# Transposing x tiles by DMA instead of on TensorE, and reordered loads, in a one-layer hybrid decoder on eight cores

## What is computed

```python
def rmsnorm(x, g):
    xf = x.astype(jnp.float32)
    y = xf * lax.rsqrt(jnp.mean(xf * xf, axis=-1, keepdims=True) + EPS)
    return (y * g.astype(jnp.float32)).astype(x.dtype)
...
    proj = jnp.einsum("btd,de->bte", xn, w_in)          # xn = rmsnorm(x, norm_attn_g), w_in 1024 x 3072
    q, k, v, gate_b, gate_c, h = jnp.split(proj, SPLITS, axis=-1)
    # three attention groups of four heads of 64: windows 128, 512, 2048 with dilations 1, 4, 16
    # group outputs weighted by their softmax denominators; beside them a gated convolution of width 3
    mixed = jnp.concatenate([attn, conv_out], axis=-1)  # [B,T,1024]
    return jnp.einsum("bte,ed->btd", mixed, w_out), new_kv, new_conv
...
        x = x + mix
        x = x + squared_relu_mlp(rmsnorm(x, norm_mlp_g[l]), w_up[l], w_down[l])   # d_ff = 4096
    y = rmsnorm(x, norm_final_g)
```

## Time and profile before

| | |
|---|---|
| median of 3 runs | 3103.34 us (3100.91 to 3105.41) |
| the profiled execution's own time | 3103.4 us |
| its span, slowest core (core 1) | 3102.0 us |
| spans of the 8 cores | 3090.5 to 3102.0 us |
| mean granted TensorE clock of the cores | 0.984 to 0.986 |
| PE busy | 2953.4 us (95%) |
| DVE busy | 1302.3 us (42%) |
| ACT busy | 1032.7 us (33%) |
| POOL busy | 198.5 us (6%) |

### The profile page before, as it was taken

One profiled execution on the slowest core, in us unless ns is written; L12 is line 12 of the kernel. 1 busy time (PEld: TensorE's weight loads), 2 busy tenths in 40 slices (PEclk: granted clock), 3 DMA queues, 4 the chain that ended last, 5 costly groups with the idle time before them and its releaser, 6 DMA issues.

```text
span 3102.0 us, 62901 instructions; the slowest of 8 cores (3090.5 to 3102.0 us)
## 1 busy us (share of the span) xinstructions
PE 2953.4 (95%) x21987; PEld 1875.4 (60%) x21987; DVE 1302.3 (42%) x2876; ACT 1032.7 (33%) x2336; POOL 198.5 (6%) x256
## 2 busy tenths in 40 slices
PE   4997899999996899999999999999999999999998
PEld 2564465564553466666666666666666666666665
DVE  5445537548443333433343333433343333333332
ACT  3244336346243322322232323222232323222232
POOL 2201201101000000000000000000000000000000
PEclk9998999999998899999999999999999999999999
DMA  7414535435135646575655655565556665544320
GB/s 166 76 47 103 126 70 145 109 78 147 32 132 173 182 104 141 138 144 125 138 129 142 144 127 134 136 144 127 136 132 145 137 131 129 136 125 97 112 68 25
DMA packets 347119, 374.71 MB, mean 121 GB/s; under 512 B 209248, under 2 KB 301440, under 8 KB 343424
## 3 DMA queue, kind: packets, MB, share of 16 engines
q1 hardware_dynamic: 268832, 216.20, 27.5%
q0 software_dynamic: 71312, 67.19, 14.1%
q10 hardware_dynamic: 6672, 87.31, 8.7%
HBM read 309.57 MB, written 176.39 MB: 157 GB/s over the span
## 4 chain that ended last, share of the span: by engine, by line
PE 87%; DVE 4%; DMA 3%; issue 3%; ACT 2%; POOL 1%; SPq 1%; another core or an unknown queue 0%; DVEq 0%; ACTq 0%; POOLq 0%
PE pp L717 29%; PE pp L728 29%; PE pp L570 13%; PE pp L678 7%; PE pp L537 4%; DMA attnT<-xn 1%; PE pp L540 1%; DMA w_in_sb<-w_in 1%; PE pp L586 1%; PE pp L515 1%; DVE Csb L970 1%; DVE xn L918 1%; DVE Csb L967 1%; PE pp L607 1%; PE pp L590 1%
## 5 line engine op out<-in xcount | busy, mean ns | idle before, releaser
L717 PE MATMUL pp<-xn1T,w_up_sb 128*128 128x256 bf16 (+1 forms) x8448 | 1067.2, 271 | 1.8 <-DVE osb L1010 1.0
L728 PE MATMUL pp<-w_down_sb,h1T 128*128 128x512 bf16 x4160 | 1052.8, 379 | 0.2 <-DVE h1T L1130 0.2
L717 PEld LDWEIGHTS pp<-xn1T,w_up_sb 128*128 128x128 bf16 x8448 | 811.8, 98 | 284.5 <-issue 11.1
L876 ACT ACTIVATE hr<-pp 128x256 bf16<-128x256 f32 (+1 forms) x1056 | 393.3, 381 | 1163.7 <-PE pp L717 1129.9
L1130 DVE TENSOR_TENSOR h1T<-hr 128x256 bf16<-128x256 bf16 (+1 forms) x1056 | 300.8, 290 | 943.7 <-ACT hr L876 882.0
L728 PEld LDWEIGHTS pp<-w_down_sb,h1T 128*128 128x128 bf16 x4160 | 403.8, 98 | 287.4 <-issue 0.3
L570 PE MATMUL pp<-xnT,w_in_sb 128*128 128x512 bf16 x2304 | 536.6, 382 | 22.5 <-DMA w_in_sb<-w_in 9.9
L570 PEld LDWEIGHTS pp<-xnT,w_in_sb 128*128 128x128 bf16 x2304 | 212.4, 98 | 267.1 <-issue 35.0
L678 PE MATMUL pp<-w_out_sb,attnT 128*128 128x512 bf16 x1040 | 249.1, 383 | 4.2 <-DMA attnT<-xn 4.2
L840 ACT ACTIVATE PT<-pp 128x1024 bf16<-128x1024 f32 x171 | 174.7, 1024 | 120.3 <-PE pp L590 118.3
L1003 DVE TENSOR_TENSOR PT<-PT,mask 128x1024 bf16<-128x1024 bf16 (+1 forms) x192 | 129.4, 674 | 187.4 <-ACT PT L840 172.0
(11 more groups left out here) (130 smaller groups left out, 1751.7 us busy)
## 6 DMA issues: line engine op xcount, KB each, us to landing
kvs<-ck ACTq DMA_DIRECT2D x128, 510.0 KB, 4.7
xt<-xp SPq DMA_DIRECT2D x64, 512.0 KB, 4.9
xtB<-xp SPq DMA_DIRECT2D x64, 512.0 KB, 4.8
yp<-xtB SPq DMA_DIRECT2D x64, 512.0 KB, 4.3
NZ<-osb SPq DMA_DIRECT2D x192, 130.0 KB, 2.0
NZt<-NZ SPq DMA_DIRECT2D x64, 390.0 KB, 6.1
kvs<-ck ACTq DMA_DIRECT2D x32, 504.0 KB, 4.3
sK<-ck POOLq DMA_DIRECT2D x52, 256.0 KB, 4.0
```

The lines of the kernel that those rows point to most:

```text
L717: ins = e.matmul(bank(v % 2)[:, 0:N], lhsT=w_up_sb[:, i // 8, kc, (i % 8) * 128:(i % 8 + 1) * 128], rhs=xn1T[T % 2][:, kc, 0:N], start=kc ...
L728: ins = e.matmul(psD[s][:, half * 512:(half + 1) * 512], lhsT=h1T[v % NH][:, s * 128:(s + 1) * 128], rhs=w_down_sb[:, i, half * 512:(half ...
L876: e.activation(out=hr[v % NHR][:, 0:N], in_=bank(v % 2)[:, 0:N], func=AF.Relu).then_inc(s_hr, 1)
```

## The change

1. x tiles from the 18th on (`k >= 17`, 48 of them) are no longer transposed on TensorE and copied by VectorE; SyncE issues a DMA transpose (`xt`) from `xn` straight into `xnT`, once the projections ahead of it in the list have ended. The reader functions `x_read` and `x_ready` wait for it, and VectorE waits for the transpose of tile k-2 before it writes `xn` again.
2. `norm_attn_g` is multiplied into the weights `w_in_sb` instead (`gw`, 8 multiplies of 128x768 for each of the four arrays, on VectorE). The first 17 tiles keep their TensorE transpose, with a plain copy behind it.
3. ScalarE squares into `junkA` instead of into `xn`; to make room, `osb` has four buffers instead of five.
4. x tiles from the 5th on are loaded only when the first `w_in` array has landed; the second array is loaded at tile 6 instead of at the start.
5. The 16 stores of `kvss` of a group become one.
6. `w_out` is loaded in group 1 of the last round; the first quarter of `w_up` later in group 2. GpSimd waits for the first two `cvT` loads before it issues the other three quarters and `w_down`.
7. For pairs 0 and 1, `attn_n` and `xn1` are transposed by TensorE (`bp`, `tp`) into PSUM bank 0 or 7; ScalarE copies the first into `attnT`, VectorE multiplies the second straight from PSUM.

```diff
 FIRST_B = [(-1, "LX", 0, 0), (-1, "LX", 0, 1), (-1, "LN", 0, 0), (0, "LN", 0, 1), (0, "LC", 0, 0), (0, "a", 0, 0),
-           (1, "b", 0, 0), (2, "LN", 1, 0), (3, "a", 0, 1), (4, "b", 0, 1), (5, "c", 0, 0, 0), (5, "LN", 1, 1),
-           (6, "c", 0, 0, 1), (8, "c", 0, 1, 0), (9, "n", 0, 0), (9, "t", 0, 0), (10, "c", 0, 1, 1), (12, "d", 0, 0),
-           (13, "n", 0, 1), (13, "t", 0, 1), (15, "d", 0, 1)]
+           (2, "bp", 0, 0), (2, "LN", 1, 0), (3, "a", 0, 1), (4, "c", 0, 0, 0), (5, "bp", 0, 1), (5, "LN", 1, 1),
+           (6, "c", 0, 0, 1), (8, "c", 0, 1, 0), (9, "n", 0, 0), (10, "c", 0, 1, 1), (11, "tp", 0, 0), (11, "d", 0, 0),
+           (13, "n", 0, 1), (14, "tp", 0, 1), (14, "d", 0, 1)]
...
     def xb(self, k):
+        if k < 17:
+            self.steps.append(("xb", dict(k=k, n=self.nring)))
...
+        else:
+            self.steps.append(("xt", dict(k=k, full=self.nproj)))
...
+            for w, first in ((1, 16), (2, 32), (3, 48)):
+                if first <= P.slot < first + 8:
+                    P.add("gw", w=w, kc=P.slot - first)
...
+            if st == 3 and g == 1:
+                P.first_wo = P.nproj
+                P.later(3, "wl", i=0)
             if st == 3 and g == 2:
                 P.first_w = P.nproj
-                P.later(3, "wl")
+                P.later(20, "wl", i=1)
...
-    NO = 5
+    NO = 4
...
+        def x_ready(W, n):
+            W.wait_ge(s_xnT, min(n, 17))
+            for i in range(max(17, n - 2), n):
+                x_read(W, i)
...
+                            if n == 4:
+                                W.wait_ge(s_gw[0], kc + 1)
...
             elif what == "skv":
-                W.wait_ge(s_stkvs, 16 * 16 * a["g"])
+                W.wait_ge(s_stkvs, 16 * a["g"])
...
                     if k >= 2:
-                        W.wait_ge(s_xT, k - 1)
-                    e.activation(out=xn[k % 2][:], in_=xt[k % 4][:], func=AF.Square,
+                        W.wait_ge(s_xn, k - 1)
+                    e.activation(out=junkA[:], in_=xt[k % 4][:], func=AF.Square,
...
-                    e.tensor_tensor(out=xnTs[:] if k == 16 else xnT[:, :, col0:col0 + 128],
-                                    in0=bank_bf(a["n"] % 2).rearrange("p (k t) -> p k t", k=8),
-                                    in1=g_attn_sb[:, :].unsqueeze(2).broadcast_to([128, 8, 128]),
-                                    op=ALU.mult).then_inc(s_xnT, 1)
+                    e.tensor_copy(out=xnTs[:] if k == 16 else xnT[:, :, col0:col0 + 128],
+                                  in_=bank_bf(a["n"] % 2).rearrange("p (k t) -> p k t", k=8)).then_inc(s_xnT, 1)
+                elif kind == "gw":
...
+                    e.tensor_scalar(out=w_in_sb[w][:, kc, :], in0=w_in_sb[w][:, kc, :], scalar1=g_attn_sb[:, kc:kc + 1],
+                                    scalar2=None, op0=ALU.mult).then_inc(s_gw[w], 1)
                 elif kind == "xn":
                     k = a["k"]
                     W.wait_ge(s_rstd, k + 1)
+                    if k >= 2:
+                        x_read(W, k - 2)
...
+            for i in range(2):
+                W.wait_ge(s_bcv[i], 16)
             for c in range(1, 4):
                 e.dma_start(out=w_up_sb[:, c, :, :], in_=w_up_v[:, :, c * 1024:(c + 1) * 1024]).then_inc(s_wu[c], 16)
...
                 if kind == "xl":
                     k = a["k"]
+                    W.wait_ge(s_ldw[0], 16)
                     W.wait_ge(s_xn, k - 3)
...
+                elif kind == "xt":
+                    k = a["k"]
+                    col0 = (XSEQ[k] % 16) * 128
+                    W.wait_ge(s_xn, k + 1)
+                    W.wait_ge(s_proj, a["full"])
+                    e.dma_start_transpose(out=xnT[:, :, col0:col0 + 128], in_=xn[k % 2][:]).then_inc(s_xTd[k % 2], 16)
...
                     W.wait_ge(s_free[a["eng"]], a["first"])
-                    for bb in range(NSB):
-                        e.dma_start(out=kvs[g][bb, WIN[g] - 8:WIN[g], :], in_=kvss[bb * 8:(bb + 1) * 8, :]).then_inc(s_stkvs, 16)
+                    e.dma_start(out=kvs[g][:, WIN[g] - 8:WIN[g], :], in_=kvss[:]).then_inc(s_stkvs, 16)
```

More of the change, by code:

```diff
@@ L187, in make_plan @@
             P.xb(k - 1)
+    for kc in range(8):
+        P.add("gw", w=0, kc=kc)
     xs_conv = spread(4, 16, 0, 14)
@@ L453, in build_nc @@
         s_ldx = [sem("ld_x%d" % i) for i in range(4)]
+        s_xTd = [sem("x_tr%d" % i) for i in range(2)]
+        s_gw = [sem("w_in_scaled%d" % i) for i in range(4)]
         s_norm, s_rstd, s_xn, s_xT, s_xnT = sem("norm_chain"), sem("rstd"), sem("xn"), sem("xT"), sem("xnT")
@@ L522, in tensor_a @@
                         W.wait_ge(s_free[eng], v)
[L523 removed]
+                    x_ready(W, a["xb"])
                     wi = w_in_sb[0] if what[-1] in "BCHu" else w_in_sb[1 + a["g"]]
[L525 to L528 removed]
+                    w = 0 if what[-1] in "BCHu" else 1 + a["g"]
+                    W.wait_ge(s_gw[w], 8 if n > 4 else 1)
                     if what in ("v", "kvt"):
@@ L637, in order_b @@
                             continue
+                        elif what in ("b", "t", "bp", "tp") and (T + dT < 2) != (what[-1] == "p"):
+                            continue
                         elif 0 <= T + dT < NT_B and (not i or i[0] < nsub(T + dT)) and (T + dT > 1 or what != "LN"):
@@ L649, in b_bank, with tr_bank @@
             return 1 if T == 0 else B_M
+        def tr_bank(T):
+            return bank_bf(7 if T else 0).rearrange("p (k t) -> p k t", k=8)
         def tr_done(W, sems, q):
-            W.wait_ge(sems[q % 2], 16 * (q // 2 + 1))
+            if q < 4:
+                W.wait_ge(s_aTe if sems is s_aT else s_xTp, q + 1)
+            else:
+                W.wait_ge(sems[q % 2], 16 * (q // 2 - 1))
         def done_x1(T):
@@ L661, in tensor_b @@
             for kind, T, i, *half in events:
-                if kind == "c":
+                if kind == "bp":
+                    q = nsubs_before(T) + i
+                    if T == 0:
+                        W.wait_ge(s_free["act"], P.nev["act"])
+                        W.wait_ge(s_free["dve"], P.nev["dve"])
+                    W.wait_ge(s_an, q + 1)
+                    if q:
+                        W.wait_ge(s_aTe, q)
+                    for kc in range(6):
+                        ins = e.transpose(out=tr_bank(T)[:, kc, :], in_=attn_n[:, kc * 128:(kc + 1) * 128], identity=ident[:])
+                    ins.then_inc(s_aTp, 1)
+                elif kind == "tp":
+                    q = nsubs_before(T) + i
+                    W.wait_ge(s_xn1, q + 1)
+                    W.wait_ge(s_aTe, 2 * T + 2)
+                    if q:
+                        W.wait_ge(s_xn1T, q)
+                    for kc in range(8):
+                        ins = e.transpose(out=tr_bank(T)[:, kc, :], in_=xn1[:, kc * 128:(kc + 1) * 128], identity=ident[:])
+                    ins.then_inc(s_xTp, 1)
+                elif kind == "c":
                     q = nsubs_before(T) + i
@@ L865, in scalar_b @@
                 n = NORM.get((kind, T, i))
-                if kind == "c" and half[0] == 1:
+                if kind == "bp":
+                    q = nsubs_before(T) + i
+                    W.wait_ge(s_aTp, q + 1)
+                    if q >= 2:
+                        W.wait_ge(s_m, 2 * (q - 1))
+                    e.activation(out=attnT[q % 2][:, 0:6, :], in_=tr_bank(T)[:, 0:6, :], func=AF.Copy).then_inc(s_aTe, 1)
+                elif kind == "c" and half[0] == 1:
                     q = nsubs_before(T) + i
@@ L1120, in vector_b @@
                     W.wait_ge(s_ldgm, 16)
-                    e.tensor_tensor(out=xr, in0=xr,
+                    e.tensor_tensor(out=xr, in0=tr_bank(T) if q < 4 else xr,
                                     in1=g_mlp_sb[:, :].unsqueeze(2).broadcast_to([128, 8, 128]), op=ALU.mult
@@ L1216, in pool @@
             for kind, a in STEPS:
-                if kind == "xc" and a["k"] in (13, 16):
-                    load_w_in(1 if a["k"] == 13 else 2)
+                if kind == "xc" and a["k"] in (6, 13, 16):
+                    load_w_in((6, 13, 16).index(a["k"]))
                 elif kind == "xc" and a["k"] == 8:
@@ L1297, in sync_a @@
                 elif kind == "wl":
-                    W.wait_ge(s_proj, P.first_w)
+                    W.wait_ge(s_proj, P.first_w if a["i"] else P.first_wo)
                     W.wait_ge(s_pre, 16 * 36)
-                    e.dma_start(out=w_out_sb[:], in_=w_out_v).then_inc(s_wo, 16)
-                    e.dma_start(out=w_up_sb[:, 0, :, :], in_=w_up_v[:, :, 0:1024]).then_inc(s_wu[0], 16)
+                    if a["i"]:
+                        e.dma_start(out=w_up_sb[:, 0, :, :], in_=w_up_v[:, :, 0:1024]).then_inc(s_wu[0], 16)
+                    else:
+                        e.dma_start(out=w_out_sb[:], in_=w_out_v).then_inc(s_wo, 16)
                 elif kind == "proj" and a["kind"] == "skv":
```

32 lines of the change are left out of this document (17 added, 15 removed), and 8 rows, old and new, of the table SLOTS.

## The result

The changed kernel takes 3072.34 us (median of 4 runs, 3069.39 to 3079.26) against 3103.6 us (3100.91 to 3105.41) beside it on the same chip: a ratio of 0.9903, 95% interval 0.9884 to 0.9922. It is faster by 31 us, where 95 were forecast, and the time lies outside the range given. The profiled execution took 3074.4 us, the span of its slowest core (core 4) is 3072.8 us. In some executions of every kernel the cores of one die have a lower granted clock and longer spans: those much longer for it are not counted, and where a profiled execution shows it (e1, e5, e9) the rows are of a core of the other die.

What follows compares the result with a forecast made beforehand. TensorE was taken as the bound, busy 2953.4 of 3102.0 us. Savings of 40 + 13 + 10 + 7.7 + 22 + 4 = 97 us from 3103.3 gave 3006.6, stated as 3008; 8-in-10 range 2980 to 3046.

Steps and rivals of the forecast that it cites:

- Part 1: x tiles from the 18th on: 29.1 us of TensorE transposes and 11 of idle go; 40 us saved, bounds 10 and 57.
- (c): Phase one: DMA transposes land as late as beside bulk loads, 22.6 us; slower than before, 3373 us; chance 0.05.
- (b): Bulk-load stall returns at NZ stores, DMA transposes land late: 3031 us, or 3050 with 8.7 us landings; chance 0.22.
- (e): Phase one: DMA transposes land in 10 us, x tiles save nothing and lose 24 us: 3070 us; chance 0.03.
- all lower bounds together: Whole kernel: every term saves only its lower bound, 29 us in all, giving 3074 us.
- Part 2: Start and first conv block: 8 us net from earlier weights, 5 of idle; 13 us saved, bounds 3 and 20.
- Part 3: Sample block: waits for sVn go as one store replaces 16; 10 us saved, bounds 5 and 15.
- Part 4: Phase-two weights at the kvt tiles: 5.96 us wait and lower-clock matmuls go; 7.7 us saved, bounds 3 and 8.
- Part 5: Last projection to first up: 38 us instead of 60, chunks waiting for the bulk; 22 us saved, bounds 8 and 28.
- Part 6: First rows of phase two: DMA transpose wait and lower clock go; 4 us saved, bounds 0 and 7.
- falsifier of conv blocks above 65 us: Conv blocks staying above 65 us would prove it wrong: VectorE's order, not the transposes, set their pace.
- that of landings above 8 us: DMA transposes into xnT: landings exceeding 8 us would prove the prediction wrong; 3 to 5 us expected.

Runs made afterwards that it cites:

- e1: Changed kernel with all x tiles transposed by TensorE again, everything else as changed: 3055.86 us, one counted run.
- e5: Changed kernel with GpSimd's 36 casting copies moved out of the stretches that prepare x tiles: ratio 0.9802, three runs of 3032.3 to 3034.3 us, one of 3060.2.
- e9: Changed kernel with casting copies moved apart and part of the bulk load behind the last attention chunk: ratio 0.981, 3032.9 to 3062.4 us.
- e14: Kernel before the change with only its casting copies moved apart: ratio 0.9999, 3100.4 to 3105.4 us.
- e6: Changed kernel with casting copies moved apart and all x tiles transposed by TensorE: ratio 0.9833, 3049.1 to 3050.5 us.
- e13: Changed kernel with casting copies moved apart, three xn buffers and conv-block tiles prepared by slot 14: ratio 0.9737, 3018.8 to 3024.4 us.
- e8: Changed kernel with w_up's third and fourth quarters loaded behind the last attention chunk: ratio 0.9892, 3060.0 to 3079.3 us.
- e10: Changed kernel with each casting copy cut in two, halves issued every third slot instead of wholes every sixth: ratio 0.9898, 3065.5 to 3076.5 us.

## Why the prediction was wrong, and where it was right

**Part 1 failed in its price of the new wait: a transpose taken to land in 3.2 us, with about 1 us of stall for a block's last tile.** Behind it stands the sentence "Nothing takes the place of this work on a computing engine", taken as if nothing took its place at all. The work left TensorE and VectorE (VectorE is busy for 54 us less), but it went to the DMA engines, at 1.8 us of all sixteen a tile. I had checked the landing of one such transpose where the second phase runs it (3.2 us) and the DMA share of the stretches before the change (0.33 to 0.74), and not added the one to the other (rival (c) even gives 58 to 75% for windows whose rows go down to 0.33): after it the share is 0.73 to 0.86. There the transposes meet the casting copies. Both suffer: a copy lands after 6.5 to 6.8 us before the change (medians, 474 to 580 us) and 8.2 to 9.9 after it (two copies, 500 to 560 us), and 5.4 in e5 (two copies). What followed were landings with a median of 5.3 us and a maximum of 12.0, SyncE issues of up to 7.2 us, waits of 29.6 us on TensorE and 43.7 us on VectorE, which had no term in the sum, and a conv block 2 at a clock of 0.86. -40 was predicted, +12 measured, which is outside the bounds of 10 to 57 us saved as well. It is the meeting that costs: the copies alone cost nothing (e14; 6 us in the changed kernel with TensorE's transposes, by e1's one run and e6), the transposes without them gain 16 us over TensorE's (e5 against e6) and with three buffers and two slots of margin 28 (e13 against e6), and with both in the same place they lose 16 (the changed kernel against e1).

Why a store's issue takes SyncE 6.64 us is not shown by any run; what is shown is that it happens within some 4 us of a copy's issue and is gone when the copies are elsewhere, even though x loads and transposes share the queue as before. Nor does a run tell how much of the loss came of the late landings and how much of SyncE's long issues.

Of the rivals, (b), (c) and (e) priced late landings by one number for all tiles, 8.7, 22.6 or 10 us. The time came out at rival (e)'s 3070, and within 2 us of the 3074 of all lower bounds together, and both by luck. Rival (e)'s mechanism was not at work: the median landing was 5.3, and the loss came, as the trace reads, of the few late ones at places without margin, of VectorE's 21 waits for a buffer, and of SyncE's order behind them. The DMA figure of the Trainium skill (VectorE: DVE Perf Modes, the three transpose paths) put a tile at 10.5 us by estimate; the 48 landings here, 2.7 at the least and 5.3 in the middle, disagree with it as a price of the transpose itself. Another page of the Trainium skill (Advanced Engine Details and Errata, X-Bar Transpose) has transposes by DMA as fast as regular ones. By SyncE's queue on the profile's pages of e5 and e6, taking the rest of the queue as the same in both (30.9% of 3030.7 us against 28.7% of 3048.6) 48 tiles of 262 KB took 61 us of the sixteen engines, 205 GB/s, and the queue's other 214 MB 875 us, 245 GB/s: nearly so, a sixth slower. So the rule nearly holds and was of no help, since it speaks of rate and the loss was one of sharing. (The whole queue's difference comes to 1.3 us a tile, the windows' to 1.8; no run says which is nearer.)

**Part 2** (-13): -9.4. The start came as worked out (first projection at 22.7 us for the 22 of the sum, not the 20 to 21 of the signs), conv block 1 gave 2 us, not 5: its transposes stayed on TensorE, and it still waits for `xn`.

**Part 3** (-10): -9.4, right; the waits for `sVn` shrank to single us.

**Part 4** (-7.7): right. The stretch is 11.1 us shorter, of which 7.9 lie from the `kvt` tiles to the QK tiles of group 2; the other 3.3, at round 4's first V tiles, where a wait of 3.5 us for a V copy is gone, were not foreseen, and no experiment took them apart.

**Part 5** (-22): the mechanism was right, the size was off: -14.3. TensorE waits for `osb`, `osb` for `NZ` stores, as foreseen. The term that was mis-sized is the bulk's end, taken at 27 us behind the last projection. The bulk loads of the changed kernel, from a window of 960 to 1040 us:

```profile
w_up_sb<-w_up_b POOLq DMA_DIRECT2D x3, 2048.0 KB, 22.3
...
w_down_sb<-w_down_b POOLq DMA_DIRECT2D x1, 768.0 KB, 32.8
```

GpSimd issues them only from 966.9 us on, 8 us behind the last projection; the last quarter of `w_up` lands at about 1000 us and the 768 KB of `w_down`, issued at 969.6, at 1002.4: 44 us behind the last projection. TensorE did not come half way and stand, either: it waited ten times for `osb`, 2.8 us at the longest, and the chunks trickled along with the stores, at a clock of 0.68. TensorE was busy for 5.8 of the 10 us from 970 on, and from 980 to 1000 the clock is 0.50, 1.2 GHz. With less bulk in front the same chunks run at 0.85 (e8).

**Part 6** (-4): +2.5. The wait for `attnT` is gone, and TensorE waits 4.7 us for the second part of `w_down` instead. GpSimd issues that part 2.6 us behind the first `up` (2.7 before), but it lands after 14.0 us where it took 8.6. Two x loads of 512 KB now go out 1 us ahead of it, where they stood 10 us behind it; that these are the cause is not tested. I had asked at part 5 what would be late next, and not here.

The sum by the measured terms: +11.8 - 9.4 - 9.4 - 7.9 - 14.3 + 2.5 - 3.3 + 0.6, rounded 29 us. Of the missing 64 us part 1 makes up 52. My falsifier of conv blocks above 65 us came true at 72.6, with another cause than the one I had attached to it (it was set against windows of 68 to 72 us, and conv block 2 by itself took 62.8 before); that of landings above 8 us came true for some tiles.

## What to carry to other kernels

Work that is moved from an engine to DMA is a load on the sixteen DMA engines: add its share to that of the very windows it will run in, and look for what else is issued there that could be elsewhere. Here, moving 36 background copies to other slots, free for the kernel before, turned a loss of 16 us into a gain of 16. And a remedy that shows nothing while another limit holds (buffers, margin) is to be tried again once that is gone: beside the copies three buffers and an earlier end brought nothing, and with the copies moved 0 and 2 to 3 us singly and 12 together.

## What was not expected of the hardware

- Beside casting copies of 512 KB, DRAM to DRAM, in GpSimd's queue, not only transfers in SyncE's queue are late but SyncE's issuing: 0.32 us became 6.64 for a store, 1.2 became 7.2 for a transpose. With the copies elsewhere a transpose's issue took 2.4 us at most (e5). With TensorE's transposes and the copies in place a store's took up to 4.2 us (e1), so the transposes by DMA are not needed for it. One long issue of the changed kernel, 6.0 us for a `convp` store at 797 us, has no copy within 50 us and stays unexplained. Halving the copies made the waits on transposes no shorter (29.6 and 43.7 us on TensorE and VectorE, 31.9 and 51.4 in e10).
- A transpose of 128x1024 by DMA from SBUF to SBUF costs SyncE 1.2 us to issue, four times a plain store's 0.32, and 1056 packets of 248 bytes (311760 - 261072 packets for 48 tiles, e5 against e6).
- The mean granted clock of the whole span is set in its first third: to 1024 us it is 0.95 in the changed kernel and to 1016 us 0.97 in e6, and behind that 1.00 in both. The changed kernel's longest wait of TensorE past the start is 13.8 us, e6's 4.4 us.
